# Two tiles of a depthwise convolution as chunk products on restacked data, in a six-mixer transformer kernel

## The chip, the core and the metric

The kernel runs on one NeuronCore of a Trainium2 chip. The metric is the time of one launch in device microseconds, the median of three runs. The engines are named as the profile names them: PE is TensorE (matmuls; PEld its weight loads), DVE is VectorE, ACT is ScalarE, POOL is GpSimd, SP is SyncE, which here only issues transfers. All engines run their own instruction streams in order, and semaphores join them.

## The reference

A stack of four mixer layers is followed by two blocks of mixer and gated feed-forward network, 512 positions of width 1024. The change concerns the first mixer of the second part, stage "e" of the kernel: differential attention with four heads beside a causal depthwise convolution.

```python
def conformer_conv(g, dw_w, dw_b, ln_g, ln_b):
    u = g[..., :CONV_CHANNELS] * jax.nn.sigmoid(g[..., CONV_CHANNELS:])
    y = lax.conv_general_dilated(
        u, dw_w[:, None, :].astype(u.dtype), window_strides=(1,),
        padding=[(CONV_WIDTH - 1, 0)], dimension_numbers=('NWC', 'WIO', 'NWC'),
        feature_group_count=CONV_CHANNELS) + dw_b
    return jax.nn.silu(layernorm(y, ln_g, ln_b))

def even_mixer(t, layer_idx, w_in, ..., w_out, cos, sin):
    proj = t @ w_in
    y_a = diff_attention(proj[..., :3 * DIFF_WIDTH], layer_idx, lq1, lk1, lq2, lk2, subln, cos, sin)
    y_b = conformer_conv(proj[..., 3 * DIFF_WIDTH:], dw_w, dw_b, ln_g, ln_b)
    return jnp.concatenate([y_a, y_b], axis=-1) @ w_out
```

There are 512 convolution channels, so four tiles of 128, and 31 taps. Each attention head has 128 channels (two halves of 64 whose softmaxes are subtracted), and each of its four query blocks of 128 positions attends the blocks up to its own.

## The kernel before

**Layout and stages.** Activations lie transposed: channels on the 128 partitions, the 512 positions along a row. Eight stages follow each other: a0, b, c, a1, e, f0, o, f1. Weights come in 456 units of 128x1024 (512 KB) in one stream. SP loads a unit into `raw`, ACT rounds it into `w_high` (`split_high`, line 277), DVE makes the remainder `w_low` (`split_low`, line 284), and PE multiplies in three passes (high by high, high by low, low by high). Splits run three units ahead of the product. A unit is 24 products of 512 columns.

**Stage e** is written as 50 slots that every engine walks through in order (`for slot in range(E_SLOTS)` in `e_tensor`, `e_scalar`, `e_vector` and `e_gpsimd`). Two slots make one weight unit of the plan `E_PLAN` (line 1612). A unit ("a", m) gives the raw channels of convolution tile m, ("b", m) its gate, ("v", n) the values, ("q", 2h) and ("q", 2h+1) the queries and keys of head h. The order of units is a0 b0 a1 b1 v0-v3 q0 q1 a2 b2 q2 q3 a3 b3 q4-q7, then the eight output units.

- Rotary embedding: two slots after a q unit begins, PE multiplies the tile by a rotation (line 1755), POOL multiplies by the cosine (line 2098), DVE by the sine (line 2004) and adds (line 2007).
- Attention: `E_SCORE_SLOT` gives each of the 16 blocks (four per head) its slot. In slot s PE makes the scores (line 1787), DVE masks them with a memset (line 2026), takes the maximum (2028) and scales it (2032), and ACT takes two exponentials (1885). In slot s+1 DVE mixes the two halves (lines 2014 to 2020). In slot s+2 PE transposes (1770) and ACT copies (1879), and in slot s+3 PE multiplies by the values (1764). Within a slot DVE does the mix of block s-1 before the softmax of block s. After a head's last block ACT copies the output twice (1892, 1895), PE sums columns (1819) and spreads the reciprocal root (1833), and DVE makes the head's output (2081).
- Convolution: DVE gates a tile (line 1968), in the odd slot after its b unit. Tiles 0 and 1 and the first 21 taps of tile 3 are DVE instructions of 128x512, two or three per slot (`E_COUNTS`, line 1989). Tile 2 and the other ten taps of tile 3 are f32 products on PE, one per tap, of a diagonal matrix and the shifted tile (line 1803, slots in `E_DIAGONALS`). ACT builds each diagonal two slots earlier in a ring of eight (line 1911). DVE adds the parts (`join`, line 1942), and an ACT copy (line 1915) takes the first 15 taps of tile 2 away in between.
- Layer norm over the four tiles: the mean in slot 44 (line 1811), squares and sums in slots 45 to 47, scaling in slot 49, SiLU behind the slots (line 1928).

POOL does nothing else in this stage than the eight rotary products. `o_prepare` on DVE, in stage a0, makes constants for stage o in the same way as the new `e_prepare`.

## Time and profile before

| | before |
|---|---|
| median of 3 runs | 3019.84 us |
| lowest and highest | 3019.76, 3021.64 us |
| the profiled execution | 3030.46 us, span 3028.7 us |
| PE busy in it | 2924.4 us, 97% of the span |
| DVE, ACT, POOL busy | 1714.8, 1061.6, 213.1 us |
| TensorE clock granted, mean | 0.981 of full speed |

Stage e runs from about 1750 to 2000 us of the span. The slots around the change begin on PE at about 1816 (slot 21), 1828 (24), 1862 (28), 1886 (33), 1917 (37), 1938 (41) and 1957 (44). The trace gives start and duration of each instruction; an f32 product (not rounded) shows as two records that overlap, and so does its weight load. Where PE waits for another engine, the row says for which. A time in a row is a place in the span; the rows themselves stand in the section below.

### The profile page before, as it was taken

The page shows a single profiled execution, that of the slowest core. Times are in us where ns is not written, and L with a number is a line of the kernel's source. Part 1 is how long each engine was busy: PE and PEld are TensorE (multiplying, and loading weights), DVE is VectorE, ACT ScalarE, POOL GpSimd, SP SyncE. Part 2 cuts the span into 40 slices and gives each one's busy share as a digit, 9 for nine tenths or more (in the row PEclk, how much of TensorE's full clock was granted, in tenths as well). Part 3 has the DMA queues.
Part 4 walks back from the last instruction along what each step waited for, and adds up shares of the span by engine and source line. Part 5 has one row for each costly group of instructions (what it writes and reads, how often), then busy time and mean ns, then how long its engine had stood idle before and what let it go on. Part 6 is the DMA issues. An engine that isn't in the chain of part 4 may idle for free.

```text
span 3028.7 us, 38678 instructions
## 1 busy us (share of the span) xinstructions
PE 2924.4 (97%) x14206; PEld 2413.4 (80%) x14206; DVE 1714.8 (57%) x2639; ACT 1061.6 (35%) x1601; POOL 213.1 (7%) x256
## 2 busy tenths in 40 slices
PE   7999999999999999999999999989999988999998
PEld 6888888888888778878888876588888875788887
DVE  5555535765576666654455576646444576464445
ACT  4332323443344332224332323434232345442222
POOL 1000000000000000001000000015502110110001
PEclk9999999999999999999999999989999999999999
DMA  4322232122221233332232331013333310223332
GB/s 146 97 96 85 92 104 77 56 63 77 78 62 56 63 105 95 95 97 90 90 97 83 97 102 45 29 55 106 92 95 96 99 63 16 62 85 96 96 97 90
DMA packets 70400, 252.14 MB, mean 83 GB/s; under 512 B 7808, under 2 KB 9856, under 8 KB 69632
## 3 DMA queue, kind: packets, MB, share of 16 engines
q1 hardware_dynamic: 68112, 241.89, 25.9%
q10 hardware_dynamic: 2016, 7.96, 0.7%
q8 instruction: 87, 1.43, 0.2%
q0 software_dynamic: 144, 0.52, 0.0%
q14 instruction: 41, 0.34, 0.0%
HBM read 248.25 MB, written 2.10 MB: 83 GB/s over the span
## 4 chain that ended last, share of the span: by engine, by line
PE 84%; DVE 8%; ACT 4%; issue 3%; POOL 1%; DMA 0%; DVEq 0%; ACTq 0%; POOLq 0%
PE ps L297 17%; PE ps L299 17%; PE ps L298 17%; PE ps L568 2%; PE ps L569 2%; PE ps L570 2%; ACT w_high L277 2%; DVE w_low L284 2%; PE ps L779 1%; PE ps L780 1%; PE ps L781 1%; PE ps L1803 1%; PE ps L853 1%; PE ps L591 1%; PE ps L839 1%
## 5 line engine op out<-in xcount | busy, mean ns | idle before, releaser
L284 DVE TENSOR_TENSOR w_low<-raw,w_high 128x1024 fp32r<-128x1024 f32 x456 | 565.8, 1246 | 420.8 <-ACT w_high L277 413.7
L297 PE MATMUL ps<-h_high,w_high 128*128 128x512 f32 x1872 | 737.8, 394 | 6.4 <-DVE arena L1464 3.0
L299 PE MATMUL ps<-h_high,w_low 128*128 128x512 f32 x1872 | 729.9, 390 | 0.0
L298 PE MATMUL ps<-h_low,w_high 128*128 128x512 f32 x1872 | 729.4, 390 | 0.0
L277 ACT ACTIVATE w_high<-raw 128x1024 fp32r<-128x1024 f32 x456 | 477.9, 1051 | 450.9 <-PE ps L299 204.0
L297 PEld LDWEIGHTS ps<-h_high,w_high 128*128 128x128 f32 x1872 | 352.3, 188 | 78.3 <-DVE arena L1464 3.4
L299 PEld LDWEIGHTS ps<-h_high,w_low 128*128 128x128 f32 x1872 | 351.8, 188 | 73.9
L298 PEld LDWEIGHTS ps<-h_low,w_high 128*128 128x128 f32 x1872 | 352.3, 188 | 70.1
L297 PE MATMUL ps<-y_high,w_high 128*128 128x512 f32 x640 | 250.4, 391 | 0.6 <-DVE y_low L1938 0.3
L298 PE MATMUL ps<-y_low,w_high 128*128 128x512 f32 x640 | 249.1, 389 | 0.0
L299 PE MATMUL ps<-y_high,w_low 128*128 128x512 f32 x640 | 249.0, 389 | 0.0
L325 POOL TENSOR_TENSOR root<-root,ssq 128x512 f32<-128x512 f32 x24 | 32.9, 1372 | 1691.5 <-ACT ssq L313 1690.0
L297 PEld LDWEIGHTS ps<-y_high,w_high 128*128 128x128 f32 x640 | 120.1, 188 | 28.0 <-DVE y_low L686 2.0
L299 PEld LDWEIGHTS ps<-y_high,w_low 128*128 128x128 f32 x640 | 120.1, 188 | 25.0
L298 PEld LDWEIGHTS ps<-y_low,w_high 128*128 128x128 f32 x640 | 120.2, 188 | 24.5
L568 PE MATMUL ps<-w_high,h_high 128*128 128x512 f32 x256 | 102.6, 401 | 11.4 <-DVE w_low L284 11.4
L569 PE MATMUL ps<-w_low,h_high 128*128 128x512 f32 x256 | 101.8, 397 | 0.0
L570 PE MATMUL ps<-w_high,h_low 128*128 128x512 f32 x256 | 101.6, 397 | 0.0
L1556 ACT ACTIVATE y_high<-full 128x512 f32 (+1 forms) x44 | 27.8, 632 | 192.2 <-DVE full L1590 192.2
L779 PE MATMUL ps<-w_high,h_high 128*128 128x512 f32 x192 | 76.8, 400 | 3.2 <-DVE x L520 2.1
L780 PE MATMUL ps<-w_low,h_high 128*128 128x512 f32 x192 | 75.8, 395 | 0.0
L781 PE MATMUL ps<-w_high,h_low 128*128 128x512 f32 x192 | 75.7, 394 | 0.0
(443 smaller groups left out, 4526.0 us busy)
## 6 DMA issues: line engine op xcount, KB each, us to landing
raw<-stream SPq DMA_DIRECT2D x456, 512.0 KB, 3.6
table<-tables_in ACTq DMA_DIRECT2D x5, 1088.0 KB, 6.5
x<-x_in ACTq DMA_DIRECT2D x8, 256.0 KB, 8.3
x_out<-x SPq DMA_DIRECT2D x16, 128.0 KB, 1.7
const<-const_in SPq DMA_DIRECT2D x1, 673.0 KB, 7.9
arena<-ssm_in POOLq DMA_DIRECT2D x1, 512.0 KB, 5.8
params<-params_in ACTq DMA_DIRECT2D x1, 287.0 KB, 6.7
```

The costliest lines, as they stand in the source:

```text
L277: nc.scalar.activation(w_high[:, u.slot], raw[:, u.raw], ACT.Copy).then_inc(weights_high, 1)
L284: nc.vector.tensor_tensor(w_low[:, u.slot], raw[:, u.raw], w_high[:, u.slot].bitcast(F32), ALU.subtract).then_inc(weights_low, 1)
L297: nc.tensor.matmul(bank, wh, high[:, k], start=k == 0, stop=False)
L298: nc.tensor.matmul(bank, wh, low[:, k], start=False, stop=False)
L299: mm = nc.tensor.matmul(bank, wl, high[:, k], start=False, stop=k == tiles - 1)
L325: nc.gpsimd.tensor_tensor(root[:], root[:], (sq, ssq)[m % 2][:], ALU.add).then_inc(norm_gathered, 1)
L568: nc.tensor.matmul(bank, hh, wh, start=k == 0, stop=False)
L569: nc.tensor.matmul(bank, hh, wl, start=False, stop=False)
L570: mm = nc.tensor.matmul(bank, hl, wh, start=False, stop=k == KD - 1)
L779: nc.tensor.matmul(bank, hh, wh, start=k == 0, stop=False)
L780: nc.tensor.matmul(bank, hh, wl, start=False, stop=False)
L781: mm = nc.tensor.matmul(bank, hl, wh, start=False, stop=k == KD - 1)
```

## The change

Convolution tiles 2 and 3 go to PE in another form, and DVE keeps the taps of tiles 0 and 1 alone (62, two per slot in slots 5 to 24, three in slots 25 to 30, two in 31 and 32). The 512 positions of a tile are cut into 128 chunks of four. The tile is restacked so that a partition holds (position within the chunk, channel of a group of 32) and a row holds (group, chunk). A group's convolution is then a sum of nine f32 products of a 128x128 matrix and 128 chunk columns, shifted by one chunk each: 36 products of 128 columns for a tile. The matrices are made on POOL, four in one 128x512 instruction, in a ring of four areas; the taps that go into them are laid out once, by `e_prepare` on DVE in stage a0.

The restacking goes through DRAM on POOL's own DMA queue: one transfer of 256 KB out, a wait until it has landed, four of 64 KB in. The result, copied with the bias by ACT (four copies of 128x128), is restacked back: four transfers out, a wait, one in. Tile 2's transfers in stand in slot 25 and out in slot 33, tile 3's in 29 and 35. The layer norm reads tiles 2 and 3 from the restacked place with a stride (`e_conv`).

The order of units changes: a3 b3 now stand directly behind a2 b2 and ahead of q2 q3. Head 1's blocks move from slots 29 to 32 into 33 to 36, so that the twelve blocks of heads 1 to 3 are in slots 33 to 44 without a break.

```diff
-        E_SCORE_SLOT = [21, 22, 23, 24, 29, 30, 31, 32] + list(range(37, 45))
-        E_END_SLOT, E_SUM_SLOT, E_HEAD_SLOT = (27, 35, 43, 47), (28, 36, 45, 48), (29, 37, 46, 49)
+        E_SCORE_SLOT = [21, 22, 23, 24] + list(range(33, 45))
+        E_END_SLOT, E_SUM_SLOT, E_HEAD_SLOT = (27, 39, 43, 47), (28, 40, 45, 48), (29, 41, 46, 49)
-        E_DIAGONALS = {25: (2, 0, 4), 26: (2, 4, 8), 27: (2, 8, 12), 28: (2, 12, 15), 33: (2, 15, 19), 34: (2, 19, 23),
-                       35: (2, 23, 27), 36: (2, 27, 31), 41: (3, 21, 25), 42: (3, 25, 28), 43: (3, 28, 31)}
+        E_CHUNK, E_QUADS, E_BACK = 4, 4, 8
+        E_CHUNKS, E_MATRICES = T // E_CHUNK, E_QUADS * (E_BACK + 1)
+        E_BATCH, E_AREAS = 4, 4
+        E_FILTER = {28: (0, 0, 18), 29: (0, 18, 36), 31: (1, 0, 18), 32: (1, 18, 36)}
+        E_EVICT_SLOT, E_FILTER_BANK = (30, 33), (2, 4)
+        E_STACK_SLOT, E_SPREAD_SLOT = (25, 29), (33, 35)
+        E_BUILD = {18: range(0, 4), 28: (4, 5), 29: (6, 7, 8), 30: (9, 10), 31: (11, 12, 13), 32: (14, 15, 16), 33: (17,)}
...
@@ e_tensor
+                if slot in E_FILTER:
+                    tile, n0, n1 = E_FILTER[slot]
+                    if n0 == 0:
+                        pe.wait_ge(e_moved, E_MOVES * (tile + 1))
+                        pe.wait_ge(e_exp, (6, 8)[tile])
+                    for n in range(n0, n1):
+                        q, k = divmod(n, E_BACK + 1)
+                        batch = E_BATCHES * tile + n // E_BATCH
+                        if n % E_BATCH == 0 or n == n0:
+                            pe.wait_ge(e_built, batch + 1)
+                        at = n % E_BATCH * P
+                        mm = nc.tensor.matmul(ps[:, E_FILTER_BANK[tile], q * P:(q + 1) * P], e_area[batch % E_AREAS][:, at:at + P],
+                                              e_stack[tile][:, q, k:k + E_CHUNKS], start=k == 0, stop=k == E_BACK)
+                        if n % E_BATCH == E_BATCH - 1:
+                            mm.then_inc(e_filtered, 1)
...
@@ e_scalar
+                if slot in E_EVICT_SLOT:
...
+                    for q in range(E_QUADS):
+                        nc.scalar.activation(full[:, 1 - tile, q * P:(q + 1) * P], ps[:, E_FILTER_BANK[tile], q * P:(q + 1) * P],
+                                             ACT.Identity, bias=e_bias[:, 2 * q + tile:2 * q + tile + 1]).then_inc(e_joined, 1)
...
@@ e_vector, the gate
+                    if m < 2:
+                        out, sg, u = e_u[:, m, PADT:], e_sg[m % 2][:], e_u[:, m, PADT:]
+                    else:
+                        out, sg, u = e_gate, by_chunk(e_sg[m % 2][:]), by_chunk(full[:, m - 2])
+                    if m == 3:
+                        dve.wait_ge(e_moved, 16)
...
@@ e_gpsimd
+                if slot in E_STACK_SLOT:
+                    tile = E_STACK_SLOT.index(slot)
+                    pool.wait_ge(e_gated, tile + 3)
+                    pool.dma_start(e_turns[tile].rearrange("p i c -> p (i c)"), table[:, 3 * T:4 * T]).then_inc(e_moved, 16)
+                    pool.wait_ge(e_moved, E_MOVES * tile + 16)
+                    turned = e_turns[tile].rearrange("(q h) i c -> i h q c", q=E_QUADS)
+                    for i in range(E_CHUNK):
+                        pool.dma_start(e_stack[tile][32 * i:32 * i + 32, :, E_BACK:], turned[i]).then_inc(e_moved, 16)
+                for batch in E_BUILD.get(slot, ()):
+                    tile, n = divmod(batch, E_BATCHES)
+                    if batch >= E_AREAS:
+                        pool.wait_ge(e_filtered, batch - E_AREAS + 1)
...
+                    nc.gpsimd.tensor_tensor(e_area[batch % E_AREAS].rearrange("p (e h) -> p e h", e=per),
+                                            e_mask.unsqueeze(1).to_broadcast(shape), taps.unsqueeze(2).to_broadcast(shape),
+                                            ALU.mult).then_inc(e_built, 1)
+                if slot in E_SPREAD_SLOT:
+                    tile = E_SPREAD_SLOT.index(slot)
+                    pool.wait_ge(e_joined, E_QUADS * (tile + 1))
+                    pool.wait_ge(e_moved, E_MOVES * (tile + 2))
+                    spread = e_turns[2 + tile].rearrange("(q h) i c -> i h q c", q=E_QUADS)
+                    for i in range(E_CHUNK):
+                        rows = full[32 * i:32 * i + 32, 1 - tile].rearrange("p (q c) -> p q c", q=E_QUADS)
+                        pool.dma_start(spread[E_CHUNK - 1 - i], rows).then_inc(e_moved, 16)
+                    pool.wait_ge(e_moved, E_MOVES * (tile + 2) + 16 * E_CHUNK)
+                    pool.dma_start(e_back[tile], e_turns[2 + tile]).then_inc(e_moved, 16)
...
-    units = conv(0) + conv(1) + [unit_wide(w_in, 2 * kk, D) for kk in range(4)] + head(0) + conv(2) + head(1)
-    units += conv(3) + head(2) + head(3)
+    units = conv(0) + conv(1) + [unit_wide(w_in, 2 * kk, D) for kk in range(4)] + head(0) + conv(2) + conv(3)
+    units += head(1) + head(2) + head(3)
```

What now stands on the engines. POOL before, all of stage e (line 2098 is the rotary product; the rows around it belong to norms):

```order
L325 TENSOR_TENSOR root<-root,sq 128x512
L2098 TENSOR_TENSOR arena<-arena,table 128x512 x8
L333 TENSOR_TENSOR root<-root,ssq 128x512
```

One row of eight rotary products was all. POOL now, slots 25 to 32: line 2133 is the rotary product, 2137 and 2141 are the transfers of the restacking, 2151 the builds of matrices:

```order
L2133 TENSOR_TENSOR arena<-arena,table 128x512
L2137 DMA e_turns<-table 128x512
L2141 DMA arena<-e_turns 32x4x128 x4
L2151 TENSOR_TENSOR work<-const 128x512 x2
L2137 DMA e_turns<-table 128x512
L2141 DMA arena<-e_turns 32x4x128 x4
L2151 TENSOR_TENSOR arena<-const 128x512 x2
L2151 TENSOR_TENSOR work<-const 128x512
L2133 TENSOR_TENSOR arena<-arena,table 128x512
L2151 TENSOR_TENSOR work<-const 128x512
L2151 TENSOR_TENSOR arena<-const 128x512 x2
L2151 TENSOR_TENSOR work<-const 128x512 x2
```

The first transfers are tile 2's (slot 25), two builds of slot 28 follow, and then the transfers of tile 3 stand ahead of the three builds of slot 29, all in one queue.

PE before, slot 28: the end of a half unit, a rotary product (1755), the last three diagonal products of the first part (1803) and the column sums of head 0 (1819):

```order
L1748 MATMUL ps<-h_low,w_high 128x512
L1749 MATMUL ps<-h_high,w_low 128x512
L1755 MATMUL ps<-arena,const 128x512
L1803 MATMUL ps<-arena,work 128x512 x3
L1819 MATMUL ps<-const,sq 128x1 x4
L1747 MATMUL ps<-h_high,w_high 128x512
L1748 MATMUL ps<-h_low,w_high 128x512
L1749 MATMUL ps<-h_high,w_low 128x512
```

PE now, slot 28: the end of a half unit, the first 18 chunk products of tile 2 (1813) and the same sums (1834):

```order
L1761 MATMUL ps<-h_high,w_high 128x512
L1762 MATMUL ps<-h_low,w_high 128x512
L1763 MATMUL ps<-h_high,w_low 128x512
L1813 MATMUL ps<-arena,work 128x128 x8
L1813 MATMUL ps<-arena 128x128 x8
L1813 MATMUL ps<-arena,work 128x128 x2
L1834 MATMUL ps<-const,sq 128x1 x4
L1761 MATMUL ps<-h_high,w_high 128x512
```

The diagonal products of 512 columns have become products of 128 columns, and the sums of head 0 stay behind them.

DVE now, slots 28 and 29: the taps (2020), the two small instructions that finish the sums of head 0 (2083, 2087), and the gate of tile 3 (2007):

```order
L285 TENSOR_TENSOR w_low<-raw,w_high 128x1024
L2020 SCALAR_TENSOR_TENSOR arena<-arena,params 128x512 x3
L2083 SCALAR_TENSOR_TENSOR arena<-arena 128x4
L2087 SCALAR_TENSOR_TENSOR arena<-ps,arena 128x4
L2007 SCALAR_TENSOR_TENSOR table<-rstd,full 128x128x4
L2011 RECIPROCAL arena<-arena 128x4
L2020 SCALAR_TENSOR_TENSOR arena<-arena,params 128x512 x3
```

The gate of tile 3, formerly behind the blocks of head 1, now follows directly on the instruction that needs the sums of head 0.

## Rows read from the trace of the kernel before

**Rows 1.** Busy time by stretch: us, PE, PEld, DVE, ACT, POOL, PEclk, DMA, GB/s
```profile
1780.00:1800.00 20.00, 20.00 (x90) 16.56 (x89) 19.40 (x26) 4.25 (x4) 0.00 (x0) 1.00 0.31 100
...
1860.00:1880.00 20.00, 20.00 (x85) 13.44 (x84) 10.97 (x21) 7.62 (x13) 1.26 (x1) 1.00 0.12 32
...
1940.00:1960.00 20.00, 16.75 (x62) 8.39 (x62) 11.10 (x28) 9.57 (x29) 0.00 (x0) 0.91 0.09 27
```

**Rows 2.** Chain of waits, 1840 to 1870, and all records of line 1803
```profile
1841.52 6.49 PE ps L1803 x8
...
1848.01 0.23 PE ps L1747
...
1852.73 3.44 PE ps L1803 x8
...
1858.92 0.89 PE ps L1764 x8
...
L1803 PE MATMUL ps<-arena,work x82: 590/592/1219, 1841.5 to 1953.6; 128*128 128x512 f32 x82
```

**Rows 3.** Taps of line 1989, and the product that waits at 1811
```profile
L1989 DVE SCALAR_TENSOR_TENSOR arena<-arena,params x83: 721/752/1768, 1768.6 to 1941.9; 128x512 f32<-128x512 f32 x83
...
1811.62 0.47 PE L1747 MATMUL ps<-h_high,w_high 128*128 128x512 f32 x1 [2.44 <-DVE ssq L2004]
```

**Rows 4.** Timeline of ACT and DVE, slots 23 to 25
```profile
1833.30 1.27 ACT L1911 ACTIVATE work<-const,params 128x128 f32<-128x128 f32 x4
...
1840.77 0.69 DVE L1968 SCALAR_TENSOR_TENSOR arena<-root,arena 128x512 f32<-128x512 f32 x1
```

**Rows 5.** POOL instructions of 128x512: groups by form, and line 2098
```profile
L2743 POOL TENSOR_TENSOR arena<-arena,small 128x512 f32<-128x512 f32 x4 | 5.0, 1252 | 0.3
...
L2743 POOL TENSOR_TENSOR arena<-const,work 128x512 f32<-128x512 f32 x2 | 3.1, 1527 | 36.1 <-DVE const L2896 36.0
...
L2098 POOL TENSOR_TENSOR arena<-arena,table x8: 1265/1468/1890, 1806.5 to 1935.8; 128x512 f32<-128x512 f32 x8
```

**Rows 6.** The page's DMA issues, and POOL's own issue
```profile
x_out<-x SPq DMA_DIRECT2D x16, 128.0 KB, 1.7
...
arena<-ssm_in POOLq DMA_DIRECT2D x1, 512.0 KB, 5.8
...
L2761 POOL DMA_DIRECT2D arena<-ssm_in x1: 722/722/722, 2059.9 to 2059.9; - x1
```

**Rows 7.** Timeline of DVE and ACT, the four blocks of head 3
```profile
1944.72 0.17 DVE L2026 MEMSET ps<- 64x128 f32 x1
...
1946.19 0.20 ACT L1885 ACTIVATION_READ_ACCUMULATOR arena<-ps,arena 128x1 f32 x1
...
1949.38 0.15 DVE L2014 RECIPROCAL arena<-arena 128x1 f32<-128x1 f32 x1
...
1950.20 0.17 DVE L2026 MEMSET ps<- 64x128 f32 x1
...
1953.34 0.17 DVE L2026 MEMSET ps<- 64x128 f32 x1
...
1956.45 0.62 DVE L2020 SCALAR_TENSOR_TENSOR arena<-arena 128x384 f32<-128x384 f32 x1
...
1960.35 0.17 DVE L2026 MEMSET ps<- 64x128 f32 x1 [3.28 <-PE ps L1787]
...
1963.95 0.75 DVE L2020 SCALAR_TENSOR_TENSOR arena<-arena 128x512 f32<-128x512 f32 x1
```

**Rows 8.** The page's weight splits, and a table load of ACT
```profile
L284 DVE TENSOR_TENSOR w_low<-raw,w_high 128x1024 fp32r<-128x1024 f32 x456 | 565.8, 1246 | 420.8 <-ACT w_high L277 413.7
...
L277 ACT ACTIVATE w_high<-raw 128x1024 fp32r<-128x1024 f32 x456 | 477.9, 1051 | 450.9 <-PE ps L299 204.0
...
1966.69 1.28 ACT L1902 ACT_TABLE_LOAD   x1
```

**Rows 9.** Busy time by stretch at the start of the kernel
```profile
86.00:108.00 22.00, 22.00 (x98) 18.20 (x97) 9.66 (x10) 9.15 (x14) 0.00 (x0) 1.00 0.43 134
```

More of the change, by code:

```diff
@@ L267, in build @@
         v_stats_r = sem("v_rstd")
+        e_moved = sem("e_moved")
         def split_high(act, u):
@@ L647, in a_vector_part @@
                     o_prepare(dve, c)
+                if name == "a0" and c == 2:
+                    e_prepare(dve)
             dve.wait_ge(v_squared, 16 * (a + 1))
@@ L1939, in low @@
                                         ALU.subtract).then_inc(y_low_done, 1)
-            def join(m):
-                nc.vector.tensor_tensor(e_acc[:, m], e_acc[:, m], ps[:, e_tap_bank(m)], ALU.add).then_inc(e_joined, 1)
             nc.vector.memset(e_u[:, :, 0:PADT], 0.0)
+            for tile in range(2):
+                nc.vector.memset(e_stack[tile][:, :, 0:E_BACK], 0.0)
             lam = par("lambda", 0, 4 * DIFF_DIM).rearrange("p (c q d) -> p c q d", c=2, q=2)
```

155 lines of the change are left out of this document (79 added, 76 removed).

## The prediction

> **What bounds the kernel now.** I read the busy time by stretch first. TensorE (PE) is busy 97% of the span, and in most of the stage "e", the only one that the change rewrites, it has no gap: 20.0 of 20 us at 1860 [rows 1]. But it isn't bound alone. Around 1780 VectorE (DVE) is busy 19.4 of 20 us beside it, and from 1940 on PE is down to 16.75 of 20: there the attention blocks set the pace. The chain of waits then shows what PE does: half a weight unit is twelve products at 0.23 us (2.7 us), a 512-column f32 product costs 3.44/4 = 0.86 us at full clock and 6.49/4 = 1.62 us just after an idle stretch, and four 128-column f32 products cost 0.89 us, so one costs 0.22 [rows 2]. So work taken off PE is worth its time in slots 25 to 36, and nothing in slots 37 to 44, where a block's softmax, exponentials and mix go to and fro between DVE and ACT.
>
> **Removed and added on PE.** Out go 41 diagonal products (82 records at 0.59, two to a product) [rows 2]: 40 x 0.86 and, for the first four, 3 us more at the lower clock, 38.2 us with the 41st. In come 72 products of 128 columns, 72 x 0.22 = 16 us. Were PE the only limit, 22 us would be gained. It isn't, so I walk the stage in four stretches.
>
> **Stretch 1, slots 5 to 21: -3.0 us.** 21 of the 83 taps at 0.75 us leave DVE, and eight of them leave slots 8 to 15, 6 us. The PE stall of 2.44 us at 1811.6, which waits for a late DVE product, goes, and with it the slow clock behind it (some 2 us) [rows 3]. Given back: four matrices are now built on POOL in slot 18, ahead of the next rotary product, 4 x 1.4 us. POOL is then busy until about 1 to 1.5 us after that product is wanted. 4.4 - 1.4 = 3.0.
>
> **Stretch 2, slots 21 to 25: -1.2 us.** DVE and ACT set this one, unchanged but for ACT's four diagonal builds at 1833.3 (1.27 us), which stand ahead of a weight split that DVE waits for [rows 4]. The gate of tile 2, which ended at 1841.5 [rows 4], ends at 1841.5 - 4.2 = 1837.3.
>
> **Stretch 3, slots 25 to 33: POOL paces it.** Prices of a matrix build (128x512, both inputs broadcast): the nearest POOL rows are 1.25 (one operand broadcast), 1.53 as the mean of two (both broadcast), and 1.47 median, 1.89 at most for the rotary product of this stage [rows 5]. I take 1.4 with the gap, nearest to the broadcast rows, and bound it by 1.1 and 2.0. Prices of the transfers: an issue holds POOL 0.72 us; landing takes 1.7 us for 128 KB written to DRAM by another queue and 5.8 us for 512 KB read by POOL's [rows 6]. I take 3.0 from issue to landing for 256 KB out, between them and nearer the write, and 2.0 for the last 64 KB in; bounds 1.7 and 5.8 for each.
> The Trainium skill ("DMA: Bandwidth & Descriptors", Anatomy of one DMA) gives such a transfer about 2.0 us fixed plus its bytes at 436 GB/s. An estimate by it for 256 KB is 2.6 us, and the sum would gain 0.4 us more; the rows lie on both sides of it, 1.7 where it gives 2.3 and 5.8 where it gives 3.2.
> Now the walk, in the new kernel's time. Behind the gate (1837.3) come three taps and a mix (3.4 us), then on PE a transpose, two half units and an attention product, and 1 us of slow clock: PE is at the first filter at 1848.5. The restacked tile 2 has landed by 1837.3 + 3.0 + 4 x 0.72 + 2.0 = 1845.2, hidden. Eighteen products: 1852.5; the column sums of head 0: 1853.3. DVE stands in slot 28 behind these sums, so tile 3's gate ends only at 1854.2. POOL takes tile 3's transfers first and the builds 6, 7 and 8 behind them: write landed 1857.2, four issues 1860.1, builds 1861.5, 1862.9, 1864.3. PE wants build 6 at 1857.3 and leaves the filter at 1865.2. Rest of head 0, half unit, 1.5 us of slow clock, rotary product: 1871.2. POOL: its own rotary product 1872.7, builds 9 to 13 until 1879.7. PE: filter 1880.1, half unit, rotary 1883.7. POOL: rotary 1885.2, builds 14 to 17 until 1890.8. PE: 1891.7, half unit, scores of head 1 at 1894.8. Without waiting for POOL the same PE work (33.4 us from 1848.5) would end at 1881.9: POOL costs 12.9 us.
>
> **Stretch 4, slots 33 to 45: three heads back to back.** In the trace of before one block of head 3 costs, from the memset to the end of the mix, 1.7 + 0.8 = 2.5 us (width 128), 3.1, 3.7 and 4.35 us [rows 7]; 13.5 per head. A weight split in between is 1.05 + 1.25 us [rows 8], two rotary sums on DVE 2 x 1.4. Head 1: 13.5 + two splits 4.6 + rotary 2.8 + the eviction that delays ACT 1.2 = 22.1. Head 2: 13.5 + one split 2.3 + 1.4 (the other rotary lies under an exponential) + sqrt with its table load 1.28 [rows 8] and root 0.4 = 18.9. Head 3: 13.5 + split 2.3 + product, rounding and remainder of head 1's output 2.0 + copies and product ahead of the last block 2.65 = 20.4. Together 61.4 us; PE needs about 19 us per head here and stays under it, and POOL's two spreads (five transfers each, 6 to 8 us) lie in slots 33 and 35, where its rotary products are late by a microsecond at most. End of the last mix: 1894.8 + 0.2 + 61.4 = 1956.4, before 1964.7 [rows 7]: -8.3.
>
> **The rest.** The layer norm of tiles 2 and 3 now reads and writes with a stride; the same count of instructions at the same sizes. I take +0.3, bounds 0 and +2. The 36 preparing instructions on DVE at the start of the kernel are small copies (some 6 us); DVE is busy 9.66 of 22 us there while PE has no gap [rows 9], and the remainders are made three units ahead, so nothing. Would that cover fail, 6 us. ACT loses 41 builds and an eviction and gains eight short ones; only what stretch 2 and head 1 name is on the path. **Sum: -8.0 us.** The profiled execution (3030.46 us, span 3028.7) lies 10.6 us above the median of the runs, 3019.84; the difference is taken as it is: 3030.5 - 8 there, 3011.8 at the median.
>
> **Rivals.**
> *POOL keeps pace* (builds of 1.1 us or less beside landings of 2 us, or PE finds them made). The 12.9 us of stretch 3 go too: 3011.8 - 12.9 = 2999. For it: POOL idles for nearly all of stage e before. Against it: PE uses a matrix batch up in 0.89 us, and no 128x512 row on POOL is so short [rows 5].
> *The queue costs what its slowest rows say*: every landing 5.8 us and every build 2.0. Tile 2 would then be restacked 3.3 us after PE wants it, tile 3's builds start 2.8 us later, twelve builds in series cost 12 x 0.6 = 7.2 more, the four in slot 18 2.4 more; with the stride's 2 us, 17.7 us: 3029.5, slower. It decides from 8 us of added cost on. For it: the rotary product reaches 1.89; against: the row of 5.8 is twice the bytes and other transfers run beside it.
> *Nothing gained*: stretch 3 goes as forecast but PE, idle from slot 34 to 44, is granted the lower clock there (0.91 already between 1940 and 1960 [rows 1]), and products, scores and rotary steps enter the chain at twice their time, 0.7 us a slot over eleven slots: 3019.5.
> That the products are not taken off can't be: the order shows 72 in place of 41.
>
> **How the numbers follow.** Forecast 0.47, POOL keeps pace 0.13, nothing gained 0.22, slow queue 0.18. A difference of under 0.2% (6 us) can't be told from none. The forecast's own range is 3007 to 3017, so 0.36 of it is faster and 0.11 within; of the slow queue 0.14 is slower and 0.04 within, of nothing gained 0.19 within and 0.03 slower. Faster 0.49, same 0.34, slower 0.17. The range 2998 to 3026 leaves out part of both outer cases, 0.05 below and 0.13 above.
>
> **What would show it.** Right: PE waits for POOL's builds some 4 us in slot 29 and 8 us over slots 31 and 32; the write's landing is near 3 us, a build near 1.4; the stall at 1811 is gone; first scores of head 1 near 1895, last mix near 1956. Wrong: no wait on builds (then 2999), a landing or a build over 2 us in series (then no gain), or a wait of PE ahead of the first filter product.

## The result, and the profile after

The changed kernel takes **3031.93 us** (median of six runs, 3029.09 to 3034.51), the kernel before beside it 3019.8 us. The ratio is 1.0039, interval 1.0026 to 1.0052: slower, where 3011.8 and faster was forecast, and above the range's end of 3026. The profiled execution after took 3029.09 us.

The head of the page of the kernel after:

```profile
span 3027.3 us, 38824 instructions
...
PE 2911.9 (96%) x14268; PEld 2419.8 (80%) x14268; DVE 1712.1 (57%) x2654; ACT 1052.1 (35%) x1567; POOL 244.6 (8%) x294
```

PE is busy 12.5 us less than before in a span that is only 1.4 us shorter, so it waits 11 us more. Before's profile was of an execution of 3030.46 us, far above its median, so the experiments begin with new profiles of both, taken on one chip: **before_again** (3023.52 us) and **after_again** (3034.25 us). These tables use them. A boundary is the start of the DVE split of a weight unit (line 284 before, 285 after; number of the 456): 272 lies just ahead of stage e, 304 in its tail, 376 in stage o, 388 behind the clock's steps in it.

| profile | 0 to 272 | 272 to 304: stage e | 304 to 376: f0 | 376 to 388: in o |
|---|---|---|---|---|
| before, as in the rows ahead | 1725.9 | 328.9 | 403.2 | 167.2 |
| before_again | 1724.7 | 322.6 | 403.2 | 166.7 |
| after | 1718.7 | 330.3 | 403.1 | 171.0 |
| after_again | 1724.1 | 328.7 | 404.7 | 171.2 |

The columns say three things. Stage e of the profile that the forecast was built on is 6.3 us longer than that of before_again. The changed stage e is 6 to 8 us longer than the latter. And 4 to 4.5 us are lost in stage o, which the change doesn't touch. (The first column differs by up to 7 us between the profiles, of one kernel too, and after_again also takes 1.6 us more in f0 than after.)

The forecast's landmarks inside stage e, with after's times as they stand. Forecast times are moved by -6.6 us, since after reaches stage e that much earlier than the first profile of before:

| | forecast | after |
|---|---|---|
| end of the gate of tile 2 | 1830.7 | 1833.4 |
| first filter product of tile 2 | 1841.9 | 1843.64 |
| PE leaves the filter of slot 32 | 1885.1 | 1885.61 |
| scores of head 1 | 1888.2 | 1888.30 |
| end of head 1's last mix | 1910.5 | 1911.7 |
| end of head 2's last mix | 1929.4 | 1934.7 |
| end of head 3's last mix | 1949.8 | 1955.3 |

The gate comes 2.7 us late; from the first filter product to head 1 the walk holds within 2 us. The waits for POOL are smaller than forecast: PE waits 7.4 us for matrices in slots 28 to 32, 6.2 for those of the ring's areas in `arena` and 1.2 for those in `work`. These are the waits of the kernel after in that stretch (us in total, times, longest), then rows of the largest one with POOL at that time (start, duration, engine, line):

```profile
PEld ps L1813 <- POOL arena L2151: 7.1, 5, 3.6
PE ps L1813 <- POOL arena L2151: 6.2, 5, 3.4
PE ps L1813 <- POOL work L2151: 1.2, 3, 0.7
```

```profile
1850.24 0.60 POOL L2137 DMA_DIRECT2D e_turns<-table  x1 [2.60 <-DVE table L2007]
1852.88 2.17 POOL L2141 DMA_DIRECT2D arena<-e_turns  x4 [2.03 <-DMA e_turns<-table]
1855.06 2.06 POOL L2151 TENSOR_TENSOR arena<-const 128x512 f32<-128x512 f32 x2
1856.17 3.57 PE L1813 MATMUL ps<-arena 128*128 128x128 f32 x16 [3.37 <-POOL arena L2151]
...
1865.21 1.74 POOL L2133 TENSOR_TENSOR arena<-arena,table 128x512 f32<-128x512 f32 x1 [7.09 <-PE ps L1769]
1866.90 1.50 POOL L2151 TENSOR_TENSOR work<-const 128x512 f32<-128x512 f32 x1
```

Builds 6 to 8 stand behind tile 3's transfers, and build 9 behind a rotary product for which POOL idles 7.09 us, with its area long free.

Then head 2 takes 23.0 us where 18.9 stood. The rows of its last block, block 11:

```profile
1924.81 0.60 ACT L1910 ACTIVATE work<-ps 128x512 f32<-128x512 f32 x1
...
1925.51 0.77 PE L1778 MATMUL ps<-work,arena 128*128 128x128 f32 x2 [2.08 <-issue]
...
1926.63 2.08 PE L1799 MATMUL ps<-arena 64*128 64x512 f32 x4
...
1928.82 0.17 DVE L2058 MEMSET ps<- 64x128 f32 x1 [2.25 <-PE ps L1799]
...
1931.94 1.28 ACT L1917 ACT_TABLE_LOAD   x1
...
1933.47 0.18 DVE L2011 RECIPROCAL arena<-arena 128x4 f32<-128x4 f32 x1 [2.69 <-ACT arena L1917]
...
1933.84 1.28 ACT L1900 ACT_TABLE_LOAD   x1
1933.99 0.75 DVE L2052 SCALAR_TENSOR_TENSOR arena<-arena 128x512 f32<-128x512 f32 x1
...
1935.62 0.37 ACT L1900 ACTIVATE arena<-ps,arena 128x128 f32<-128x128 f32 x1 [0.50 <-DVE arena L2064]
```

Two things of head **1's** end stand in head 2's chain. The first is its output. By the code the first attention product of head 2 (line 1778) waits for ACT's second copy of head 1's output (line 1910); it starts 0.1 us behind that copy's end. Block 11's scores (line 1799) stand behind it on PE, and DVE waits 2.25 us for them; in before_again it doesn't wait there. The second is head 1's norm: its root needs the Sqrt table, a load of 1.28 us, and DVE's reciprocal of it (line 2011), for which DVE waits 2.69 us, stands ahead of block 11's mix. The load back to the exponential's table, 1.28 us as well, is over before block 12's first exponential, which waits for DVE. In the kernel before all this lay in slots 35 to 37, between the blocks of two heads. The Trainium skill ("ScalarE: Activation LUTs", Table sets: the hidden batching unit) puts exponential and square root into different sets, so that each change is a load; the rows agree.

Stretches of before_again (first fence) and after_again (second), columns as in [rows 1]:

```profile
1920.00:1940.00 20.00, 15.64 (x56) 8.33 (x55) 17.46 (x31) 6.82 (x22) 3.09 (x2) 0.83 0.10 27
1940.00:1960.00 20.00, 17.14 (x67) 8.62 (x66) 10.87 (x29) 10.21 (x31) 0.00 (x0) 1.00 0.09 27
```

```profile
1920.00:1940.00 20.00, 14.68 (x56) 9.51 (x56) 12.18 (x32) 9.18 (x22) 1.27 (x1) 0.65 0.09 27
1940.00:1960.00 20.00, 13.51 (x44) 7.06 (x43) 10.24 (x26) 8.10 (x23) 0.00 (x0) 0.75 0.07 27
```

With the tap products gone PE idles 6.5 of the 20 us from 1940 on, and is granted 0.65 and 0.75 of full speed where it was 0.83 and 1.00.

### The profile page after: what moved, and what is told of

Same layout as the page of the kernel before. It is cut to its first block, busy times and chain, and to the rows that moved or that the text cites. A ratio compares the mean times of both kernels' runs of the same rounds, so it can differ in the third digit from the quotient of the medians.

```text
span 3027.3 us, 38824 instructions
## 1 busy us (share of the span) xinstructions
PE 2911.9 (96%) x14268; PEld 2419.8 (80%) x14268; DVE 1712.1 (57%) x2654; ACT 1052.1 (35%) x1567; POOL 244.6 (8%) x294
## 3 DMA queue, kind: packets, MB, share of 16 engines
q0 software_dynamic: 976, 2.62, 0.3%
## 4 chain that ended last, share of the span: by engine, by line
PE 83%; DVE 9%; ACT 4%; issue 3%; POOL 1%; DMA 1%; DVEq 0%; ACTq 0%; POOLq 0%
PE ps L298 17%; PE ps L300 17%; PE ps L299 17%; PE ps L569 2%; PE ps L570 2%; PE ps L571 2%; ACT w_high L278 2%; DVE w_low L285 2%; PE ps L782 1%; PE ps L783 1%; PE ps L784 1%; PE ps L856 1%; PE ps L592 1%; PE ps L842 1%; PE ps L1387 1%
```

## The experiments

The kernel before, timed beside them on each chip, had medians of 3021.2 to 3021.7 us; ratios are to it. Line numbers in quoted rows are those of the kernel named.

**1. Both kernels again**, unchanged.

> The kernel before, unchanged, profiled once more. The profile behind the prediction was of an execution of 3030.5 us, the timed ones take 3019.8. In it, set beside the profile after, 6.6 us were already lost when stage e began. Theory A (the profiled execution was late for reasons that lie ahead of stage e, in stages b, c and a1, and stage e was as usual in it): this profile reaches the end of stage e 6 to 7 us earlier, and stage e, from its first unit to the last, lasts what it did, within 1 us. Theory B (the lateness lies in stage e and behind it too, so the prediction costed the change against a stage e that is not the usual one): stage e lasts 3 us or more less than in the first profile.

> The changed kernel, unchanged, for a second profile beside that of the kernel before on the same chip: 3029 or 3034 us, one of the two levels of its runs. If the levels are a place in the program, the two profiles differ in one stage by 5 us; if they are drift, by a little everywhere.

Measured: the table above. Theory B: stage e was late in the profile behind the prediction. Of its 6.3 us 0.8 are lost by unit 276, 1.8 more by 288 and 4.6 between 294 and 296 (0.9 come back by 304). The instructions are the same, and what differs is where half clock falls: 41.0 us of it in the stage against 30.7. The last head, for instance, takes 20.0 us from mix to mix with 6.8 us at half clock in it and 18.5 with none. From 1980 to 2000 the first profile was granted 0.74, before_again 0.91:

```profile
1980.00:2000.00 20.00, 16.04 (x70) 12.87 (x69) 9.19 (x14) 10.53 (x14) 0.97 (x1) 0.91 0.06 15
```

The two profiles of the changed kernel, of 3029 and 3034 us, differ by 5.4 us ahead of stage e and by at most 1.7 in any stretch behind it, in both directions. So in this pair the 5 us between them lie ahead of the change.

**2. e_prepare alone**, put into the kernel before.

```diff
+                if name == "a0" and c == 2:
+                    e_prepare(dve)
```

> The kernel before with one part of the change: the tap tables, masks and biases of e_prepare are laid out on DVE in stage a0, and nobody reads them. Prediction: nothing, 3019.8 within 1 us, and a0 ends when it did. Rival (DVE has no room in a0 and the splits behind are late): up to 6 us more, 3026. Rival (the instructions are free, but the program of the loops behind lies at another place and starts differently): 2 to 5 us more that stand behind a0, in b, c or later, with a0 itself unchanged.

Measured: 3023.04 us, ratio 0.9998 (0.9987 to 1.0009). It costs nothing, as forecast. (Stage e of its profile took 328.9 us, as long as in the first profile of before.)

**3. Without builds 4 to 17.**

```diff
-                            pe.wait_ge(e_built, batch + 1)
+                            pe.wait_ge(e_built, min(batch + 1, E_AREAS))
...
+                    if batch >= E_AREAS:
+                        continue
```

> The changed kernel without builds 4 to 17: the four matrices areas are filled once and all filter products read them, so both tiles' filters are wrong; the transfers, products, copies and order stay. Prediction's reading (POOL's builds cost PE 12.9 us of waits, and all of it comes back): 3018 to 3020, from 3031.9. Rival (the filters start when the transfers have landed, and PE's time won in slots 28 to 32 is given back in slots 33 to 44, where the chain of DVE and ACT, and the low clock behind it, set the pace): 3026 to 3030, with heads 1 to 3 taking longer by what the filters gained.

Both filters are wrong in it. Measured: 3019.75 us, 0.9993 (0.9983 to 1.0003). Stage e takes 321.8 us, 7 to 8.6 less than after: the waits for POOL come back in full, and heads 2 and 3 take 1 us more (37.2 us from first to last mix, 36.2 in after). Head 1's first mix comes 9 to 10 us earlier, more than the 7.4 us of waits, so the builds cost something besides them (see stretch 1 below). But with them gone the kernel is only where the kernel before is. That the prediction's sum would then be 2999 shows that about 20 us of its gain were missing elsewhere.

**4. Less PE work in slots 41 to 43 of the kernel before.**

```diff
+                        if m == 3 and j > E_HALF:
+                            continue
...
```

> The kernel before with nine of tile 3's ten tap products left out (slots 41 to 43), so tile 3's convolution is incomplete; ACT still builds the diagonals. That takes 9 x 0.86 = 7.7 us of PE work out of the stretch between PE's last unit and the mean. The prediction's reckoning, by which PE's work there was worth its length: 3012 to 3014, from 3021.3 on this chip. Rival (from PE's last unit on, the chain of DVE and ACT through the blocks sets the time, and the tap products lay in PE's waits and kept its clock up): 3019 to 3024, nothing gained, the mean no earlier than a microsecond, and more half clock in slots 41 to 47 than the 17 us of the profile of before_again.

Measured: 3024.82 us, 1.0010 (1.0001 to 1.0020): 7.7 us of PE work less, and nothing gained; stage e took 325.8 us. The row of the first attention product of head 3, which waited 2.86 us in before_again:

```profile
1953.70 0.77 PE L1764 MATMUL ps<-work,arena 128*128 128x128 f32 x2 [5.62 <-issue]
```

It starts 0.5 us earlier than in before_again, in a run that was 0.8 us earlier at the start of the stage. PE's clock from 1940 to 1960 is 0.74 in place of 1.00:

```profile
1940.00:1960.00 20.00, 12.00 (x40) 6.54 (x41) 10.11 (x26) 9.58 (x31) 0.00 (x0) 0.74 0.09 26
```

So what the change takes off PE in slots 41 to 43 buys nothing. After has the same 5.62 us:

```profile
1947.61 0.77 PE L1778 MATMUL ps<-work,arena 128*128 128x128 f32 x2 [5.62 <-issue]
```

**5. Builds ahead of what held them.**

```diff
-        E_BUILD = {18: range(0, 4), 28: (4, 5), 29: (6, 7, 8), 30: (9, 10), 31: (11, 12, 13), 32: (14, 15, 16), 33: (17,)}
+        E_BUILD = {18: range(0, 4), 28: (4, 5, 6, 7), 29: (8, 9, 10, 11), 31: (12, 13, 14, 15), 32: (16, 17)}
```

> The changed kernel with the matrices built earlier on POOL: builds 6 and 7 ahead of tile 3's transfers, 9 to 11 ahead of the rotary product of slot 30, 12 to 15 ahead of that of slot 32. Same work. The build waits of PE (6.2 us in slots 29, 31 and 32) should nearly go. If it is the waits that cost, as in the kernel without builds: 3020 to 3024. Rival (the same time is lost further on, since POOL's rotary products of slots 30 and 32 come later): 3028 to 3032.

Measured: 3025.0 us, 1.0005 (0.9996 to 1.0015), a little above its range; stage e 323.5 us: 5 to 7 us of the 7 to 8.6 come back without any build left out (PE still waits 3.4 us for POOL). POOL was late mostly by its order, less by its speed.

**6. Idle products for the clock.**

```diff
+                if slot in (41, 42, 43):
...
+                    for k in range((4, 3, 3)[slot - 41]):
+                        nc.tensor.matmul(ps[:, 1], ones, e_acc[:, 0], start=k == 0, stop=k == (3, 2, 2)[slot - 41])
...
+                    if b == 0 and h == 3:
+                        for k in range(5):
+                            nc.tensor.matmul(ps[:, 1], ones, e_acc[:, 0], start=k == 0, stop=k == 4)
```

> The changed kernel with 15 idle products on PE (512 columns, f32, ones by a finished tile, into the bank that the mean uses later): four in slot 41, three each in 42 and 43, five ahead of the 5.6 us wait in slot 44, where the kernel before had ten tap products. They compute nothing that is read. Theory (PE's waits in slots 38 to 44 let the clock fall for 17 us, and this is what the last heads and the mean pay): with the filler the half clock between 1915 and 1990 falls from 37.5 us to under 20, and the kernel gains 2 to 5 us, 3027 to 3030. Rival (the chain of DVE and ACT alone sets the time, the clock is a symptom): within 1 us of 3031.9, or 2 to 4 us later if the filler delays the chain's own products.

Measured: 3029.5 us, 1.0024 (1.0013 to 1.0035). Half clock between 1915 and 1990 fell from 37.5 to 22.1 us, but stage e still took 330.6: head 3 took 2.4 us more (22.9), the rest of the stage 2 us less. The gain in the median is stage o's (167.3 us, see 9), so that it fell into the theory's range says nothing for the theory. PE took in 13 us more work there at a price of 2.4.

The filler stands ahead of head 3's own products, so this run can't say what a higher clock alone would do, and it leaves head 2, which ends before it, as it was (23.0 us, 14 of them at half clock). For head 2 the kernels of experiments 8 and 11 settle it. From the end of head 1's last mix to that of head 2's they run the same instructions, 23.70 us in both, in after_contiguous (first) at 0.75 of full clock and in after_fixed at 0.88:

```profile
1915.00:1938.70 23.70, 16.80 (x74) 11.38 (x74) 14.03 (x33) 10.76 (x27) 2.53 (x2) 0.75 0.08 22
1910.50:1934.20 23.70, 14.93 (x74) 9.78 (x73) 14.02 (x33) 10.69 (x27) 2.53 (x2) 0.88 0.09 22
```

So the low clock is not what makes head 2 long.

**7. The same convolution in the old order of units**: q2 q3 ahead of a3 b3, scores, ends and banks nearly as in the kernel before. The builds and DVE's taps lie in other slots too, and in the first of the two runs the units of tile 3 and head 1 have each other's weights.

```diff
+        E_FILTER = {33: (0, 0, 18), 34: (0, 18, 36), 40: (1, 0, 18), 41: (1, 18, 36)}
+        E_EVICT_SLOT, E_FILTER_BANK = (35, 42), (2, 0)
+        E_STACK_SLOT, E_SPREAD_SLOT = (25, 35), (36, 42)
+        E_BUILD = {21: range(0, 4), 33: (4, 5, 6, 7), 34: (8, 9), 35: (10, 11), 37: (12,), 40: (13, 14), 41: (15, 16, 17)}
...
```

> The chunk products, transfers and strided layer norm of the changed kernel with the order of the kernel before: q2 q3 ahead of a3 b3, head 1 in slots 29 to 32, tile 2's products in slots 33 and 34, tile 3's in 40 and 41, builds 0 to 3 in slot 21 behind the two rotary products. Theory (the form of the convolution is good, and what costs is the order, which takes all PE work out of the last slots and puts three heads behind it): PE loses 41 x 0.86 = 35 us of taps and gets 16 us of chunk products; the part that falls ahead of slot 37, 31 x 0.86 - 8 = 19 us, is all PE's time there and comes back less 3 to 6 us of new waits, while slots 37 to 44 stay at the chain's pace: 3004 to 3012. Rival (the form itself costs what it saves, by transfers that PE and DVE wait for, the strided layer norm, or a lower clock): 3018 to 3028.

> The kernel after_old_order once more with the weight stream laid out in its order too (there the units of tile 3 and head 1 had each other's weights). The same instructions in the same order: 3006 to 3014 again, median near 3010.5, faster than the kernel before by 0.3 to 0.5%. If the order of units in the stream mattered to the time at all, it would differ by more than 2 us.

Measured: 3010.41 us, 0.9954 (0.9937 to 0.9970), and 3010.54, 0.9964 (0.9950 to 0.9978), stage e 310.9 and 309.5 us. With head 1 between two convolution tiles as before, the mixes of blocks 8 to 15 span 33.1 us where after needs 36.2, and, counted from the start of the stage, the last mix comes 18 and 19 us earlier than in after_again. Some 15 to 16 of these are there when head 2's first mix starts (172 and 173 us into the stage, 188 in after_again, 192 in before_again); 7.4 of them can be the waits for POOL's matrices, which these two kernels don't have.

**8. The layer norm over contiguous tiles**: POOL, idle then, copies the restacked tiles into place.

```diff
+                if slot == 37:
+                    for tile in range(2):
+                        pool.wait_ge(e_moved, E_MOVES * (tile + 3))
+                        pool.wait_ge(e_filtered, 2 * E_BATCHES)
+                        nc.gpsimd.tensor_copy(by_chunk(e_acc[:, 2 + tile]),
+                                              e_back[tile].rearrange("p i c -> p c i")).then_inc(e_built, 1)
...
```

> The changed kernel with a layer norm over contiguous tiles: in slot 37, where it is idle, POOL copies the two restacked tiles into place (two copies of 128x512), and the mean, centring, squares, scaling and SiLU read and write 512 neighbouring positions as in the kernel before. Prediction's term (the stride costs 0.3, at most 2 us): 3029.6 to 3031.9. Other reading, from the rows (with the stride the mean's four products took 5.5 us at full clock where 3.7 stood before, two squares 1.0 each where 0.63, two SiLUs 1.3 where 0.8, the scaling 0.65 more in all): the last 36 us of the stage get 3 to 4 us shorter, and the mean products take 3.7; 3027.5 to 3029.

Measured: 3026.12 us, 1.0015 (1.0005 to 1.0024), below both ranges. From the last mix to the product of the last attention channel it is 29.5 us, where after has 31.4 and after_again 31.8. Groups of after_again from 1950 to 2000 (SiLU, squares, scaling), then of this kernel to 1996:

```profile
L1942 ACT ACTIVATE full<-arena,params 128x512 f32<-128x512 f32 x4 | 4.2, 1059 | 0.0
L1937 ACT ACTIVATE work<-arena 128x512 f32<-128x512 f32 x4 | 3.2, 846 | 6.2 <-PE ps L1858 6.2
L2105 DVE TENSOR_TENSOR arena<-arena,ps 128x512 f32<-128x512 f32 x4 | 3.1, 849 | 5.1 <-PE ps L1842 5.1
```

```profile
L1942 ACT ACTIVATE full<-arena,params 128x512 f32<-128x512 f32 x4 | 3.2, 804 | 0.0
...
L2105 DVE TENSOR_TENSOR arena<-arena,ps 128x512 f32<-128x512 f32 x4 | 2.5, 682 | 4.7 <-PE ps L1842 4.7
L1937 ACT ACTIVATE work<-arena 128x512 f32<-128x512 f32 x4 | 2.4, 623 | 6.5 <-PE ps L1858 6.5
```

2.4 us less in these three. The mean's products, at full clock with the stride (after_filler) and without (before_again), by their lines:

```profile
L1833 PE MATMUL ps<-arena,const x8: 592/864/1051, 1955.7 to 1960.2; 128*128 128x512 f32 x8
```

```profile
L1811 PE MATMUL ps<-arena,const x8: 592/592/697, 1955.9 to 1959.0; 128*128 128x512 f32 x8
```

From first start to last end that is 5.5 against 3.7 us. From the last mix to the end of the stage it is 100.1 us, where after and after_again have 104.5 and 103.3. The rest of its gain in the median is again stage o's, 167.0 us. Stage e of this one profile took 329.0 us all the same: it stood 2 us later at head 1's first mix than after_again, counted from the stage's start, behind half clock that the other doesn't have.

**9. Stage o against the clock.** The same instructions took 171 us in after, after_again, after_no_builds and after_builds_ahead, 168 in the two kernels of experiment 7, and 167 in all other profiles so far. A few repeated products ahead of f0's tail move stage o in time:

```diff
+                if name == "f0" and j == 0:
...
+                    for _ in range(3):      # 5 in before_shifted
+                        nc.tensor.matmul(ps[:, banks[0]], w_high[:, Unit(first).slot, 0:P], y_high[:, 0], start=True, stop=True)
```

> The changed kernel with three products of 0.23 us repeated on PE near the end of stage f0, where it waits for nothing, so that all of stage o comes 0.7 us later in relation to the granted clock. In four profiles of kernels with the changed order stage o's first part (splits 376 to 388) took 171 us, with the half clock 5.7 us behind split 379 for 13.7 us; in those with 167 us it began 8.6 to 9.0 us behind it, for 6.8 us, with the same instructions. Theory (which of the two comes depends only on when stage o begins against the steps of the clock): the two stretches of this profile are 167 and 6.8 us, and the kernel, though it does 0.7 us more work, is 3 us faster than the changed kernel, 3028 to 3029.5. Rival (something of the change itself, data or memory, slows stage o): 171 us again, 3032 to 3033.

> The kernel before with five such products repeated at the same place, so stage o begins 1.1 us later against the clock's steps. Theory: stage o's first part goes from 167 to 168 to 171 us and the kernel loses 1.1 us for the products and 1 to 4 on top, 3024 to 3027 against 3021.6. Rival: 167 us again, 3022.5 to 3023.

Measured: after_shifted 3028.04 us, 1.0024 (1.0014 to 1.0034), this part of stage o 167.2 us; before_shifted 3027.89, 1.0017 (1.0007 to 1.0026), 171.1 us. Stage o went as the theory said both times. before_shifted's median is 0.9 us above its range: f0 took 2.4 us more in its profile than in before_again, where the five products are 1.15. The same window of 20 us in before_again, before_shifted, after_again and after_shifted, in this order:

```profile
2495.00:2515.00 20.00, 17.38 (x62) 10.07 (x60) 15.38 (x44) 8.54 (x22) 0.00 (x0) 0.83 0.08 27
```

```profile
2495.00:2515.00 20.00, 17.52 (x42) 9.86 (x43) 12.38 (x33) 6.39 (x15) 0.00 (x0) 0.66 0.09 27
```

```profile
2495.00:2515.00 20.00, 16.54 (x40) 9.45 (x38) 10.74 (x30) 7.95 (x16) 0.00 (x0) 0.66 0.14 35
```

```profile
2495.00:2515.00 20.00, 15.75 (x48) 9.11 (x48) 11.50 (x32) 8.11 (x17) 0.00 (x0) 0.83 0.18 48
```

A granted clock of 0.66 is 13.7 us at half speed, 0.83 is 6.8. Each kernel changed sides by a shift of about a microsecond. The Trainium skill ("TensorE: Matmul & The Clock Gate", Part 1: The HAM clock gate) says that the gate's observation runs free and does not reset with the program; the four rows agree.

**10. Head 1's root without a table load.**

```diff
-                    nc.scalar.activation(e_root, e_arg, ACT.Sqrt).then_inc(e_sub_root, 1)
+                    nc.scalar.activation(e_root, e_arg, ACT.Copy if summed == 1 else ACT.Sqrt).then_inc(e_sub_root, 1)
```

> The changed kernel with head 1's root taken by a copy in place of Sqrt, so that head 1's output is wrong and ACT loads no table for it in slot 40 and none back to the exponential (2 x 1.28 us) in the middle of head 2's blocks, where in the kernel before head 1's norm lay in slots 35 and 36, between the blocks of two heads. In the profile after, the mixes of blocks 10 and 11 are 8.05 us apart, against 4.23 in that of before. Theory (the norm of head 1 now stands in the chain of the last eight blocks): the gap falls to 5.5 us, the mixes of blocks 4 to 15 span 55 us (57.8), and the kernel gains 2 to 3 us, 3029 to 3030. Rival (the chain waits for PE at half clock there, not for the tables): within 1 us of 3031.9.

Measured: 3029.31 us, 1.0024 (1.0014 to 1.0034); stage e 328.4 us against 328.7, stage o's part 171.3. The median lies in the theory's range, but not by its mechanism. The mixes of blocks 10 and 11 came 6.6 us apart (8.1 in after_again), the whole of blocks 4 to 15 fell by 0.9 only, and nothing of it was left at the end of the stage. So the table loads are worth 1.4 us. The forecast for head 2 has 1.28 for one of them, so they are not what head 2 is over it by.

**11. All repairs in the new order**: experiments 5 and 8, and builds 0 to 3 in slot 21.

```diff
+        E_BUILD = {21: range(0, 4), 28: (4, 5, 6, 7), 29: (8, 9, 10, 11), 31: (12, 13, 14, 15), 32: (16, 17)}
...
```

> The changed kernel, in its own order of units, with what the runs so far name put right: builds 0 to 3 behind the second rotary product (slot 21, from 18), 6 to 17 ahead of the transfers and rotary products that held them up, and the contiguous layer norm. If the three add up (3.1 of the stall at 1809, 6.8 of build waits, 3 to 4 of strides) to 3031.9: 3018 to 3021, that is, no more than the kernel before, since heads 1 to 3 back to back keep their 58 us from first to last mix. Rival (the order is not the bound and the fixes show up whole ahead of the chain too): 3012 or less.

Measured: 3016.7 us, 0.9984 (0.9975 to 0.9994), stage e 320.7 us: the fixes add up, a little better than expected (1.3 us below the range), and this order ends 6 us above the old one of experiment 7, which still has the strided layer norm. In both the builds lie in better places; here PE still waits 3.9 us for them, there not at all.

**12. All repairs in the old order**, and DVE's taps spread thinner.

```diff
+        E_COUNTS = {**{n: 2 for n in range(5, 21)}, **{n: 1 for n in range(21, 25)}, **{n: 2 for n in range(25, 29)},
+                    **{n: 1 for n in range(29, 33)}, **{n: 3 for n in range(33, 37)}, 37: 1, 38: 1}
+        E_FILTER = {33: (0, 0, 18), 34: (0, 18, 36), 39: (1, 0, 18), 40: (1, 18, 36)}
...
```

> The order of the kernel before with chunk products, contiguous layer norm, tile 3's products one slot earlier (39 and 40, evicted in 41, so the transfers back land before the mean), and the 62 taps of DVE spread over slots 5 to 38, at most two in each until slot 32, so that no split waits for them. Against after_old_order: 3 to 4 us for the layer norm, 3 us for the stall at 1811, 1 to 3 us for the waits of PE for DVE's mixes in slots 23 to 29; against that 0 to 3 us if DVE's later taps delay blocks in slots 33 to 38: 3001 to 3006. Rival (POOL's rotary products in slots 38 and 40 wait behind builds 13 to 17, and DVE's sum with them): 3006 to 3012.

Measured: **2999.84 us** (2998.05 to 3002.24), 0.9929 (0.9912 to 0.9945), better than expected; stage e 305.1 us. It beats both kernels, by 0.7% and 1.1%. It changes several things at once, and no run parts them. Its last two heads are no faster than after's (37.3 us from first to last mix, 36.2 in after): the gain is in when they begin, 167 us into the stage against 188 and 189, and 184 in after_fixed.

## Why the prediction was wrong

The forecast lies 20.1 us under the measured median, and four places make that up. In the profile after, the last mix comes 5.5 us later in the stage than the walk has it (head 2 is 4.1 of that), 4.0 us more than forecast are lost behind it, where only the stride had a term, 3.8 in stage o, which had none, and 6.3 lie in the reference. That is 19.6; it can't be told closer, since profiles of one kernel differ by microseconds.

**The reference.** "The difference is taken as it is" is the first step that failed. The profile behind the sum was of a run 10.6 us above the median, and 6.3 us of that lay in stage e itself, with 10 us more at half clock. It was a rare run: of the 25 timed beside experiments 1 to 3 one came above it, and their median was 3021.3. Against before_again the same walk would have given a gain of under 2 us, not 8.

**Stretches 1 and 2** (-4.2 by the gate of tile 2): 1.4 measured against the same profile, and nothing against before_again, whose gate ends 103.7 us into the stage (after 104.1, after_again 103.3). The stall at 1811.6 did not go, as the prediction's signs wanted; it is 3.14 us in after. And it is not POOL's late rotary product, for which the 1.4 us stood: POOL is done with it at 1809.24, and DVE comes to its own part (line 2036) only at 1810.56. It is DVE that is late:

```profile
1794.57 3.11 DVE L2020 SCALAR_TENSOR_TENSOR arena<-arena,params 128x512 f32<-128x512 f32 x4
...
1801.60 2.51 POOL L2151 TENSOR_TENSOR work<-const 128x512 f32<-128x512 f32 x2
...
1803.12 2.99 DVE L2020 SCALAR_TENSOR_TENSOR arena<-arena,params 128x512 f32<-128x512 f32 x2
1804.07 2.95 POOL L2151 TENSOR_TENSOR arena<-const 128x512 f32<-128x512 f32 x2
1806.03 2.06 DVE L285 TENSOR_TENSOR w_low<-raw,w_high 128x1024 fp32r<-128x1024 f32 x1
1806.98 2.26 POOL L2133 TENSOR_TENSOR arena<-arena,table 128x512 f32<-128x512 f32 x1
1808.02 2.62 DVE L2020 SCALAR_TENSOR_TENSOR arena<-arena,params 128x512 f32<-128x512 f32 x2
...
1812.03 0.80 PE L1799 MATMUL ps<-arena 64*128 64x128 f32 x4 [3.14 <-DVE arena L2039]
```

Four taps take 3.11 us while POOL is idle, and two take 2.99 beside its builds and 2.62 beside its rotary product; a split takes 2.06 in place of 1.23. The forecast priced a build as POOL's time alone, and it costs DVE's as well. With these builds behind the second rotary product the stall is 0.77 us (experiments 11 and 12).

**Stretches 2 and 3.** From the first filter product on the landmarks hold within 2 us, but by errors that cancel: PE reached it 1.7 us later than forecast, waited 7.4 us for builds instead of 12.9, and was busy 34.6 us up to the end of slot 32's filter, where the walk has 30.3. A build took 1.04 to 1.50 us, 1.49 at the median (forecast 1.4), and the two lengths go with DVE: 1.04 to 1.06 in the five beside which DVE did nothing, 1.41 to 1.50 in eleven of the other thirteen. The landings stand in the page of after (columns: size, median us from issue to landing):

```profile
e_turns<-table POOLq DMA_DIRECT2D x2, 256.0 KB, 2.4
arena<-e_turns POOLq DMA_DIRECT2D x8, 64.0 KB, 2.2
e_turns<-full POOLq DMA_DIRECT2D x8, 64.0 KB, 2.0
```

3.0 and 2.0 had been taken for the first two. The estimate by the Trainium skill ("DMA: Bandwidth & Descriptors", Anatomy of one DMA), 2.6 us for the 256 KB, was nearer. What cost was the order of POOL's work, which the forecast took over as written (experiment 5).

**Stretch 4, head 2** (18.9 us): the term mis-sized most, 23.0 us measured. It had the root and its load. Missing are three delays, which the rows of after show. Block 11 took 8.2 us for 6.0, by the 2.25 us that DVE waits for its scores, behind ACT's copy of head 1's output (the rows above). Block 10 took 4.8 for 3.7: the second rotary sum was to lie under an exponential, but it waits for POOL and holds up the mix. Block 8 took 6.9 for 6.2: its scaling on DVE, 0.17 us elsewhere, took 1.15 beside POOL's rotary product.

```profile
1912.27 1.27 POOL L2133 TENSOR_TENSOR arena<-arena,table 128x512 f32<-128x512 f32 x1 [8.80 <-PE ps L1769]
1912.41 1.15 DVE L2064 TENSOR_SCALAR arena<-arena 128x2 f32<-128x2 f32 x1
...
1924.89 0.69 DVE L2039 TENSOR_TENSOR arena<-arena,ssq 128x512 f32<-128x512 f32 x1 [0.73 <-POOL arena L2133]
1925.49 0.15 DVE L2046 RECIPROCAL arena<-arena 128x1 f32<-128x1 f32 x1
```

Head 1 took 1.1 us more, head 3 20.5 against 20.4.

**The stride** (+0.3, at most 2): same count, same sizes, but not the same time. 1.8 us for the mean's products and 2.4 for squares, scaling and SiLU; of this some 2 us lie on the path ahead of the last attention channel (experiment 8), more behind it, 3.2 to 4.4 from the last mix to the end of the stage. The two gates that write in chunk order take 1.09 to 1.12 us instead of 0.69, which had no term either.

**Stage o** (no term): 4 us, by the place at which the changed stage e happens to end against the clock (experiment 9).

**The rivals.** "POOL keeps pace" was put at 2999; with the waits gone the kernel took 3019.75 (experiment 3). The slow queue's 3029.5 was nearest in size, by luck: landings took 2.0 to 2.4 us where it had 5.8, and no build over 1.50 where it had 2.0. "Nothing gained" was nearest in place: the chain in slots 34 to 44. Its cause, the lower clock, is refuted for head 2 (experiment 6); head 3 took what was forecast. What decided between the orders was stated in the prediction's first part and then not used for the order of the units: PE work is worth nothing in slots 37 to 44. The change takes the tap products out of just those slots and puts a third head behind them, so PE is done with its last half unit at 1916.9 and then waits for a chain of twelve blocks, where the old order leaves eight. "E_prepare costs nothing" was right.

**What stays open.** How much of head 2's 4.1 us would come back without the three delays (the rows show them, no run removes one), what each part of experiment 12 is worth, and what makes stage e of the unchanged kernel take 322.6 us in one run and 328.9 in another: its profiles part by where half clock falls, and nothing in them shows why it falls there.

## What to carry to other kernels

Before costing a change against a profile, see that its run is a usual one, or take two: here the reference was 6.3 us off inside the very stage. Work put on an idle engine can slow its neighbour: see what the other engine's instructions take while it is busy. Work taken from an engine pays only where that engine ends last, so choose the order of units such that its freed time lies there, and keep other chains' norms, table changes and copies out from between the blocks of a dependent chain. On an engine that runs in order, put what is ready ahead of what must wait.

## What the hardware showed beyond expectation

- DVE and POOL slow each other. Of the 62 taps of 128x512 in after, the 50 with POOL's engine idle took at most 0.75 us; of the 12 beside a POOL instruction ten took 1.42 to 1.79. In before_again three of the seven beside POOL took 1.64 to 1.76. A build on POOL took 1.04 to 1.06 us with DVE idle and mostly 1.41 to 1.50 beside it.
- A shift of 0.7 to 1.1 us in an unchanged stage turned 6.8 us of half clock into 13.7 or back, worth 4 us of 3020, in both kernels (experiment 9).
- An operand of 128x512 f32 whose neighbours in reading order lie 128 elements apart is slower on three engines: ACT's squares of such tiles took up to 1.09 us against 0.62 and SiLUs 1.33 against 0.80, four scalings on DVE (two of them with the step) 3.1 against 2.5, four f32 products on PE (two with it) 5.5 against 3.7 us.
